# Moving eight bias-strip transfers to SyncE's queue and rolling the head iterations into loops, in a fused encoder layer

## The chip, the cores and the metric

The kernel runs on one core of a Trainium2 chip. Time is device microseconds of a whole execution. Three runs of the kernel before took 2651.68, 2651.73 and 2653.3 us, median 2651.73. The engines are TensorE (PE), VectorE (DVE), ScalarE (ACT), GpSimd (POOL, unused here) and SyncE (SP, which only issues transfers).

## The reference

One layer is applied to two sequences, 512 and 256 tokens of width 2048 (768 tokens in all), with shared weights:

```python
h = rmsnorm(x, pre_norm_g)
proj = h @ w_in                      # 2048 x 13376
q, k, v, z_attn, z_ssm, xbc, dt_raw = jnp.split(proj, cuts, axis=-1)
o = dilated_attention(q, k, v, rel_bias_table)          # 16 heads of 128
attn_out = rmsnorm(o, attn_norm_g) * silu(z_attn)
ssm_out = ssd_branch(z_ssm, xbc, dt_raw, ...)           # 32 heads of 64, both directions
mix = concat([attn_out, ssm_out]) @ w_out               # 4096 x 2048
return x + rmsnorm(mix, post_norm_g)
```

The attention adds a bias per head that depends only on the distance of query and key. The SSD branch convolves its input over five tokens, applies SiLU, and scans in chunks of 128 tokens with decays.

## The kernel before, in words

All products run in two parts: each float32 operand is split into a high part, rounded by ScalarE's copy (`w_hi`, `h_hi`), and the rest, which VectorE gets by a subtraction (`w_lo`, `h_lo`). TensorE adds three products, high by high, high by low and low by high. A weight chunk is four 128 x 128 blocks; it passes through `w_raw` (loaded by SyncE's queue), ScalarE (`split_hi`, line 933), VectorE (`split_lo`, line 1375) and TensorE, in four slots.

The stages, in order:

- The input is normalised and transposed, and a table of biases by distance is multiplied out and stored to `brow_scr` in DRAM (line 374).
- The B/C stage: one tile for `dt` and eight tiles of B and C, in a loop over groups.
- The gate stage: 48 column tiles of gates and x. Four go tile by tile; the other 44 form 22 pairs (`NP`), each computed by a Strassen-like scheme of seven block products. A product has two halves, so a pair has 14 halves (`HP`); one is 4 x 3 matmuls of 384 columns. Each pair needs four raw loads of 512 KB (`load_raw`, line 403: `raw_a` in `stage`, `raw_b` to `raw_d` in `raw_qk`). The third step of VectorE's pair work (line 1761) needs `raw_b` and `raw_d`. Results go out as two stores, `c1` (line 408, from `w_raw`) and `c2` (line 413, from `osq_sum`). ScalarE may overwrite `c2_buf` in the snapshot of its step n = 6 only after the `c2` store of the pair before has landed (line 1230).
- The head iterations: 16 rounds (`iteration`), each with 12 chunks of v, q and k columns of one head on TensorE, and between them, in `slot` and `step`, the attention and SSD work of the head before. TensorE runs these rounds from a loop of two, ScalarE and VectorE from unrolled code. The waits count up with the head number, so in a loop they compare with a value that is computed from a register.
- The tail: the last head's attention and SSD without a projection beside it (`step(s, HEADS - 1, None)`), with the first pieces of the output projection (`w2_split`, `m_split_first`) between its steps; then the output projection and the final norm.

Every engine works through its own list in order. Nothing reorders it: a wait holds all that is behind it on that engine. SyncE and ScalarE each issue transfers to a queue of their own.

Before head 0 starts, each head needs a strip: 128 rows of 896 biases, row r shifted by r. `make_strips(h)` (line 1239) makes two heads' strips by one DRAM to DRAM transfer from `brow_scr` to `strip_scr`. ScalarE issues eight of them, one behind each of the pairs 0 to 7, and these pairs are unrolled on ScalarE (lines 1244 to 1249).

In the last iteration (head 15), VectorE copies the columns of head 15's parameters (`columns_of_channels`, `columns_of_heads`) and convolves its x (`convolve_xs`) at the end of step 11 (line 1820), and ScalarE applies SiLU there (line 1271). In step 11 stand the splits of k (`k_hi`, line 946; `k_lo`, line 1583), in step 10 the gated output `y` of the head before (`y_gated`, line 1691) and the six transfers that follow it on ScalarE's queue.

Of the kernel before, what the change touches and what calls it, by code (L numbers as in the profile page):

```python
# [24 lines left out]
P = 128  # L25
# [44 lines left out]
STRIP = SEQ + 3 * P  # L70
# [26 lines left out]
W_TURNS = {24: (0,), 27: (1,), 31: (2, 3)}  # L97

# [23 lines left out]
def encoder(nc, x_prompt, x_sample, pre_g, w_in, rel_table, attn_g, conv_w, conv_b, dtb_f, dtb_b,  # L122
# [7 lines left out]
    with ctx:  # L130
# [137 lines left out]
        strip_out = sem("strip_out")  # L268
# [68 lines left out]
        def _(sp):  # L337
# [37 lines left out]

            sp.wait_ge(xt_done, 2 * KT)
# [6 lines left out]
            for c in range(2, NCH):  # L383
                load_w(2 * NCH + c, COL_C, c)
            with sp.Fori(1, SSM_GROUPS) as g:
                gcol = sp.snap(g * P)
                for j, base in enumerate((COL_B, COL_C)):
                    for c in range(NCH):
                        load_w(NCH + 2 * NCH * g + NCH * j + c, gcol + base, c)
# [42 lines left out]
            with sp.Fori(1, NP - 1) as p:  # L432
                pair_transfers(p)
# [481 lines left out]
        def _(act):  # L915
# [169 lines left out]
            def step(s, a, i, ip=0):  # L1085
                if a is None and s == 0:
                    act.wait_ge(pads, 3)
                    load_xs(0)
                    act.wait_ge(strip_out, 16 * (HEADS // 2))
                    load_strip(0)  # L1090
                    load_gate(za, ZX_ZA, 0, za_in)
                    load_gate(zs, ZX_ZS, 0, zs_in)
                    load_decays(0)
# [145 lines left out]
            def make_strips(h):  # L1239
                act.dma_start(strip_scr[h * P:(h + 2) * P, :],  # L1240
                              bass.AP(brow_scr.tensor, h * BROW + P - 1, [[BROW, 2], [-1, P], [1, STRIP]])
                              ).then_inc(strip_out, 16)

            for p in range(HEADS // 2):
                pair(p, p % 2)
                make_strips(2 * p)
            with act.Fori(HEADS // 4, NP // 2) as g:
                pair(2 * g, 0)
                pair(2 * g + 1, 1)
# [15 lines left out]
            def iteration(i, ip, a, final=False):  # L1265
                for s in range(IT_CHUNKS):
# [4 lines left out]
                    if final and s == 11:  # L1271
# [3 lines left out]
            for i in range(1, HEADS):  # L1275
                iteration(i, i % 2, i - 1, final=(i == HEADS - 1))
# [69 lines left out]
        def _(dve):  # L1346
# [467 lines left out]
            def iteration(i, ip, a, final=False):  # L1814
                for s in range(IT_CHUNKS):
# [4 lines left out]
                    if final and s == 11:  # L1820
# [7 lines left out]
            for i in range(1, HEADS):  # L1828
                iteration(i, i % 2, i - 1, final=(i == HEADS - 1))
# [21 lines left out]
            for s in range(IT_CHUNKS):  # L1851
                step(s, HEADS - 1, None)
                if s == 1:
                    w2_split(0)
# [125 lines left out]
```

## Time and profile before

| quantity | value |
|---|---|
| median of three runs | 2651.73 us |
| profiled execution | 2651.68 us |
| its span | 2649.9 us |
| TensorE busy | 2531.5 us (96%) |
| VectorE busy | 1541.0 us (58%) |
| ScalarE busy | 865.2 us (33%) |
| mean granted TensorE clock | 0.978 |
| chain that ended last | TensorE 89%, DMA 5%, VectorE 3% |

The span runs from the first to the last instruction. The busy shares are averages over stages with different limits, so they do not say what one stage waits for. The chain follows the end of the span back from wait to wait. In the rows below, L is the line of the kernel, the engine names are PE, DVE, ACT and SP, a q behind an engine name is its sequencer or transfer queue, and x is a count. A granted clock of 1.00 is 2.4 GHz and 0.50 is 1.2 GHz.

### The profile page before, as it was taken

Reading aid. Unit: us, or ns where it says so; the run is one execution under the profiler, and the core shown is the slowest. Engines: PE = TensorE matmul, PEld = TensorE weight load, DVE = VectorE, ACT = ScalarE, POOL = GpSimd, SP = SyncE. Lnnn points to the kernel's source line nnn. Section 1 sums busy time; section 2 is a strip of 40 time slices with the busy share of each in tenths; the row PEclk is TensorE's granted clock in tenths of the full one; section 3 lists DMA queues with packets and bytes.
Section 4 is the critical chain, followed back from the end, with each engine's and each line's share of the span. In section 5 each row is a group of like instructions: output and inputs, shape, how many; then the busy total and the mean of one; then the engine's idle time right before and its main releaser. Section 6 shows DMA issues by size and latency. Waiting matters only on the chain.

```text
span 2649.9 us, 36450 instructions
## 1 busy us (share of the span) xinstructions
PE 2531.5 (96%) x14004; PEld 2371.0 (89%) x14004; DVE 1541.0 (58%) x2389; ACT 865.2 (33%) x1410; POOL 0.2 (0%) x4
## 2 busy tenths in 40 slices
PE   6999877888999999999999999999999799999998
PEld 6999877888999999999999999999999688888887
DVE  5556644344555553566666666666666855544447
ACT  5232322223333332433333333333333422211112
POOL 0000000000000000000000000000000000000000
PEclk9999988989999999999999999999999899999999
DMA  5224222333333336244444444444444342222215
GB/s 178 79 99 136 71 92 95 104 94 99 101 93 96 102 103 209 73 147 145 146 146 146 146 146 146 146 146 146 146 146 134 134 149 88 87 85 101 85 61 200
DMA packets 287861, 320.94 MB, mean 121 GB/s; under 512 B 15031, under 2 KB 232311, under 8 KB 283304
## 3 DMA queue, kind: packets, MB, share of 16 engines
q1 hardware_dynamic: 252855, 196.87, 24.3%
q10 hardware_dynamic: 34928, 123.10, 13.2%
q8 instruction: 41, 0.67, 0.1%
q14 instruction: 37, 0.30, 0.0%
HBM read 271.76 MB, written 55.51 MB: 124 GB/s over the span
## 4 chain that ended last, share of the span: by engine, by line
PE 89%; DMA 5%; DVE 3%; ACT 1%; issue 1%; ACTq 0%; SPq 0%; DVEq 0%
PE ps L587 30%; PE ps L785 21%; PE ps L856 19%; PE ps L567 8%; DMA raw_qk<-in_w_in 5%; PE ps L713 2%; PE ps L741 2%; PE ps L680 2%; PE ps L696 1%; PE ps L751 1%; PE ps L600 1%; DVE w_lo L1742 1%; PE ps L718 0%; DVE w_raw L1746 0%; PE ps L687 0%
## 5 line engine op out<-in xcount | busy, mean ns | idle before, releaser
L587 PE MATMUL ps<-h_hi,w_hi 128*128 128x384 f32 x1536 | 401.5, 342 | 3.3 <-issue 3.3
L587 PE MATMUL ps<-h_hi,w_lo 128*128 128x384 f32 x1536 | 391.5, 335 | 0.0
L587 PE MATMUL ps<-h_lo,w_hi 128*128 128x384 f32 x1536 | 391.5, 335 | 0.0
L1375 DVE TENSOR_TENSOR w_lo<-w_raw,w_hi 128x512 fp32r<-128x512 f32 x244 | 167.2, 690 | 340.5 <-ACT w_hi L933 335.7
L933 ACT ACTIVATE w_hi<-w_raw 128x512 fp32r<-128x512 f32 x240 | 150.2, 627 | 608.3 <-PE ps L587 383.6
L856 PE MATMUL ps<-h_hi 128*128 128x512 f32 x768 | 299.8, 390 | 1.7 <-issue 1.7
L856 PE MATMUL ps<-h_lo,h_hi 128*128 128x512 f32 x768 | 298.8, 389 | 0.0
L856 PE MATMUL ps<-h_hi,h_lo 128*128 128x512 f32 x768 | 298.8, 389 | 0.0
L587 PEld LDWEIGHTS ps<-h_hi,w_hi 128*128 128x128 f32 x1536 | 272.5, 188 | 8.1 <-issue 6.1
L587 PEld LDWEIGHTS ps<-h_hi,w_lo 128*128 128x128 f32 x1536 | 278.5, 188 | 0.0
L587 PEld LDWEIGHTS ps<-h_lo,w_hi 128*128 128x128 f32 x1536 | 277.7, 188 | 0.0
L785 PE MATMUL ps<-t_hi,w_hi 128*128 128x384 f32 x528 | 187.5, 355 | 65.9 <-DVE w_lo L1742 65.9
L785 PE MATMUL ps<-h_hi,w_hi 128*128 128x384 f32 x704 | 236.6, 336 | 2.7 <-DVE w_lo L1742 2.7
L785 PE MATMUL ps<-h_hi,w_lo 128*128 128x384 f32 x704 | 236.3, 336 | 0.0
L785 PE MATMUL ps<-h_lo,w_hi 128*128 128x384 f32 x704 | 236.1, 335 | 0.0
L1921 DVE SCALAR_TENSOR_TENSOR stage<-ps,coef,stage 128x512 f32<-128x512 f32 x168 | 123.7, 748 | 178.6 <-PE ps L856 178.6
L1742 DVE TENSOR_TENSOR w_lo<-raw_qk,w_hi 128x512 fp32r<-128x512 f32 x176 | 121.7, 691 | 154.4 <-ACT w_hi L1207 152.8
L785 PE MATMUL ps<-t_lo,w_hi 128*128 128x384 f32 x528 | 185.4, 351 | 0.0
L785 PE MATMUL ps<-t_hi,w_lo 128*128 128x384 f32 x528 | 185.2, 351 | 0.0
L856 PEld LDWEIGHTS ps<-h_hi 128*128 128x128 f32 x768 | 144.2, 188 | 31.6 <-issue 2.1
L856 PEld LDWEIGHTS ps<-h_hi,h_lo 128*128 128x128 f32 x768 | 144.1, 188 | 30.1
L856 PEld LDWEIGHTS ps<-h_lo,h_hi 128*128 128x128 f32 x768 | 144.2, 188 | 29.6
(228 smaller groups left out, 3888.3 us busy)
## 6 DMA issues: line engine op xcount, KB each, us to landing
w_raw<-in_w_in SPq DMA_DIRECT2D x240, 256.0 KB, 2.9
raw_qk<-in_w_in SPq DMA_DIRECT2D x66, 512.0 KB, 3.9
stage<-in_w_out SPq DMA_DIRECT2D x30, 1024.0 KB, 5.0
stage<-cb_scr ACTq DMA_DIRECT2D x16, 1664.0 KB, 13.4
stage<-loc_scr ACTq DMA_DIRECT2D x16, 1536.0 KB, 7.1
stage<-zx_scr ACTq DMA_DIRECT2D x32, 384.0 KB, 3.6
stage<-er_scr ACTq DMA_DIRECT2D x32, 384.0 KB, 9.4
u_scr<-stage ACTq DMA_DIRECT2D x32, 384.0 KB, 2.7
```

What stands on the lines that cost most here:

```text
L567: last = nc.tensor.matmul(ps[:, 2 * parity + b, 0:HALF_T], w, h[:, k * T + b * HALF_T:k * T + (b + 1) * HALF_T], start=(k == 0 and p == 0) ...
L587: last = nc.tensor.matmul(ps[:, 2 * parity + b, 0:HALF_T], w, h[:, k * T + b * HALF_T:k * T + (b + 1) * HALF_T], start=(k == 0 and p == 0) ...
L600: nc.tensor.matmul(ps[:, 4 + sc, :], bcT[0][:, sc * P:(sc + 1) * P], bcT[1][:, 0:SEQ], start=True, stop=True).then_inc(pcb_ready, 1)
L680: last = nc.tensor.matmul(ps[:, 4 + t, :], q[:, t * P:(t + 1) * P], k[:, 0:SEQ], start=(n == 0), stop=(n == 2))
L713: last = nc.tensor.matmul(ps[:, 5, :], v_tok[:, b * P:(b + 1) * P], pT[:, b * SEQ:(b + 1) * SEQ], start=(b == 0), stop=(b == PCH - 1))
L741: last = nc.tensor.matmul(ps[:, b, o * P:(o + 1) * P], xsc[:, pr * P:(pr + 1) * P], cb[:, pr * P:(pr + 1) * P], start=(q == 0), stop=(q == ...
L785: ins = nc.tensor.matmul(ps[:, bank, 0:HALF_T], w, h(k), start=(start and kk == 0 and q == 0), stop=(last and kk == KC - 1 and q == 2), sk ...
L856: last = nc.tensor.matmul(ps[:, bank, :], m[par][:, k * T + t * P:k * T + (t + 1) * P], w[slot][:, k * NBW:(k + 1) * NBW], start=(k == 0 a ...
L933: nc.scalar.activation(w_hi[:, c, :], w_raw[:, c, :], ACT.Copy).then_inc(w_hi_done, 1)
L1375: nc.vector.tensor_tensor(w_lo[:, c, :], w_raw[:, c, :], w_hi[:, c, :].bitcast(f32), ALU.subtract).then_inc(w_lo_done, 1)
L1742: nc.vector.tensor_tensor(w_lo[:, n_slot(n, pp), :], src, w_hi[:, n_slot(n, pp), :].bitcast(f32), ALU.subtract).then_inc(w_lo_done, 1)
L1921: nc.vector.scalar_tensor_tensor(acc[:, o:o + NBW], ps[:, n % TT, :], r, acc[:, o:o + NBW], ALU.mult, ALU.add).then_inc(acc_added, 1)
```

## The change

Four things change.

1. `make_strips` becomes a function of SyncE. The first strip transfer is issued before the B/C loop, the other seven between the pair transfers of the gate stage, and for that the first eight pair transfers are unrolled on SyncE. The semaphore is split in two.
2. ScalarE's pair loop starts at pair 2 instead of pair 8.
3. The head iterations 1 to 14 become a loop of two on ScalarE and VectorE.
4. In the last iteration the column copies, the convolution and its SiLU move from step 11 to step 10; in the tail VectorE's `w2_split(0)` moves from step 1 to step 0.

```diff
+DVE_PER_PASS = 28
@@ semaphores
-        strip_out = sem("strip_out")
+        strip_out = [sem(f"strip_out{i}") for i in range(2)]
@@ SyncE
+            def make_strips(h, done):
+                sp.dma_start(strip_scr[h * P:(h + 2) * P, :],
+                             bass.AP(brow_scr.tensor, h * BROW + P - 1, [[BROW, 2], [-1, P], [1, STRIP]])
+                             ).then_inc(done, 16)
...
+            sp.wait_ge(brow_out, 16)
+            make_strips(0, strip_out[0])
             with sp.Fori(1, SSM_GROUPS) as g:
...
             pair_transfers(0)
-            with sp.Fori(1, NP - 1) as p:
+            for n in range(HEADS // 2 - 1):
+                make_strips(2 * n + 2, strip_out[1])
+                pair_transfers(n + 1)
+            with sp.Fori(HEADS // 2, NP - 1) as p:
                 pair_transfers(p)
@@ ScalarE, head 0
-                    act.wait_ge(strip_out, 16 * (HEADS // 2))
+                    act.wait_ge(strip_out[0], 16)
+                    act.wait_ge(strip_out[1], 16 * (HEADS // 2 - 1))
@@ ScalarE, pairs
-            for p in range(HEADS // 2):
-                pair(p, p % 2)
-                make_strips(2 * p)
-            with act.Fori(HEADS // 4, NP // 2) as g:
+            pair(0, 0)
+            pair(1, 1)
+            with act.Fori(1, NP // 2) as g:
@@ ScalarE and VectorE, last iteration
-                    if final and s == 11:
+                    if final and s == 10:
@@ ScalarE, iterations (VectorE's has in addition the counter of its own steps)
-            for i in range(1, HEADS):
-                iteration(i, i % 2, i - 1, final=(i == HEADS - 1))
+            with act.Fori(0, HEADS // 2 - 1) as g:
+                iteration(2 * g + 1, 1, 2 * g)
+                iteration(2 * g + 2, 0, 2 * g + 1)
+            iteration(HEADS - 1, 1, HEADS - 2, final=True)
@@ VectorE, tail
+                if s == 0:
+                    w2_split(0)
                 if s == 1:
-                    w2_split(0)
                     m_split_first(0)
```

On SyncE, from the raw loads of pair 0's transfers to the `c2` store of pair 0 (`zx_scr<-w_raw` is the `c1` store, `zx_scr<-osq_sum` the `c2` store), there stands before:

```order
L403 DMA stage<-in_w_in 128x8x128 [waits wsum_done]
L403 DMA raw_qk<-in_w_in 128x8x128 [waits w_lo_done] x3
L408 DMA zx_scr<-w_raw 128x768 [waits comb_done]
L432 UNCONDITIONAL_BRANCH
L413 ISA [waits c21_done]
L413 DMA zx_scr<-osq_sum 128x768
```

and now:

```order
L413 DMA stage<-in_w_in 128x8x128 [waits wsum_done]
L413 DMA raw_qk<-in_w_in 128x8x128 [waits w_lo_done] x3
L418 DMA zx_scr<-w_raw 128x768 [waits comb_done]
L380 DMA strip_scr<-brow_scr 256x1x896
L423 DMA zx_scr<-osq_sum 128x768 [waits c21_done]
```

The strip stands between the two stores, and the branch into the loop is gone from here.

On ScalarE, from the end of pair 0 to the snapshot of pair 1 that waits for `c2_out`, there stands before:

```order
L1207 ACTIVATE w_hi<-raw_qk 128x512 [waits half_done,raw_in_d] x2
L1240 DMA strip_scr<-brow_scr 256x1x896
L1207 ACTIVATE w_hi<-stage 128x512 [waits half_done,raw_in_a] x2
L1207 ACTIVATE w_hi<-w_raw 128x512 [waits half_done,wsum_done]
L1215 ACTIVATE osq_sum<-ps 128x384 [waits half_done]
L1207 ACTIVATE w_hi<-w_raw 128x512 [waits half_done,wsum_done]
L1207 ACTIVATE w_hi<-stage 128x512 [waits half_done,wsum_done]
L1211 ACTIVATE w_raw<-ps 128x384 [waits half_done,c1_out]
L1207 ACTIVATE w_hi<-stage 128x512 [waits half_done,wsum_done]
L1207 ACTIVATE w_hi<-raw_qk 128x512 [waits half_done,raw_in_c]
L1211 ACTIVATE osq_sum<-ps 128x384 [waits half_done,c2_out]
L1207 ACTIVATE w_hi<-raw_qk 128x512 [waits half_done,raw_in_c]
```

and now:

```order
L1221 ACTIVATE w_hi<-raw_qk 128x512 [waits half_done,raw_in_d] x2
L1221 ACTIVATE w_hi<-stage 128x512 [waits half_done,raw_in_a] x2
L1221 ACTIVATE w_hi<-w_raw 128x512 [waits half_done,wsum_done]
L1229 ACTIVATE osq_sum<-ps 128x384 [waits half_done]
L1221 ACTIVATE w_hi<-w_raw 128x512 [waits half_done,wsum_done]
L1221 ACTIVATE w_hi<-stage 128x512 [waits half_done,wsum_done]
L1225 ACTIVATE w_raw<-ps 128x384 [waits half_done,c1_out]
L1221 ACTIVATE w_hi<-stage 128x512 [waits half_done,wsum_done]
L1221 ACTIVATE w_hi<-raw_qk 128x512 [waits half_done,raw_in_c]
L1225 ACTIVATE osq_sum<-ps 128x384 [waits half_done,c2_out]
L1221 ACTIVATE w_hi<-raw_qk 128x512 [waits half_done,raw_in_c]
```

Only the strip transfer has left the list.

On VectorE, from the split of the last k tile into the tail (`h_lo<-w_raw` is `w2_split(0)`, 128x772 the convolution, the ISA rows the reduction of the scores with the bias), there stands before:

```order
L1583 SCALAR_TENSOR_TENSOR k_lo<-ps,k_hi 128x768 [waits qk_hi_done]
L1357 COPY cur<-conv_cols 128x5 [waits y_gated,ua_stored,ys_stored]
...
L1413 TENSOR_SCALAR stage<-stage,cur 128x772 [waits xs_in,dve_seq]
L1416 SCALAR_TENSOR_TENSOR stage<-stage,cur 128x772 [waits dve_seq] x4
L1607 ISA stage,cur<-ps,stage 128x512 [waits strip_in,scores_ready]
...
L1561 TENSOR_SCALAR stage<-stage 128x3072 [waits dve_seq]
L1618 RECIPROCAL cur<-cur 128x4 [waits probs_exp,sscores_ready]
...
L1630 TENSOR_SCALAR stage<-stage,cur 128x512 x3
L1833 TENSOR_TENSOR h_lo<-w_raw,h_hi 128x2048 [waits w2_hi_done]
```

and now:

```order
L1423 TENSOR_SCALAR stage<-stage,cur 128x772 [waits xs_in,dve_seq]
L1426 SCALAR_TENSOR_TENSOR stage<-stage,cur 128x772 [waits dve_seq] x4
L1593 SCALAR_TENSOR_TENSOR k_lo<-ps,k_hi 128x768 [waits qk_hi_done]
L1617 ISA stage,cur<-ps,stage 128x512 [waits scores_ready,strip_in,ua_stored,ys_stored]
...
L1571 TENSOR_SCALAR stage<-stage 128x3072 [waits dve_seq]
L1849 TENSOR_TENSOR h_lo<-w_raw,h_hi 128x2048 [waits w2_hi_done]
L1628 RECIPROCAL cur<-cur 128x4 [waits probs_exp,sscores_ready]
...
L1640 TENSOR_SCALAR stage<-stage,cur 128x512 x3
```

The convolution now precedes `k_lo`, and `w2_split(0)` precedes the sample's scores and the normalisation.

## Rows read from the trace of the kernel before

**Rows 1.** Busy time by stretch (column header in the first line), the gate stage's two parts.
```profile
core 0: us, PE busy (x) PEld busy (x) DVE busy (x) ACT busy (x) POOL busy (x), PEclk, DMA share, GB/s
302.00:612.00 310.00, 248.61 (x1320) 246.08 (x1320) 129.23 (x168) 81.14 (x145) 0.00 (x0) 0.89 0.31 97
612.00:1023.00 411.00, 408.67 (x2328) 408.35 (x2328) 221.53 (x293) 145.53 (x252) 0.00 (x0) 1.00 0.34 104
```

**Rows 2.** Chain of waits in time, gate stage: start us, length us, what.
```profile
320.64 15.08 DMA raw_qk<-in_w_in
...
612.64 408.67 PE ps L785 x2328
```

**Rows 3.** Waits, 300 to 620 us: total us, times, longest us.
```profile
PE ps L785 <- DVE w_lo L1742: 65.9, 9, 7.8
```

**Rows 4.** Timeline of ScalarE's queue, second strip: start us, length us, what.
```profile
357.94 0.61 ACTq L1240 DMA_DIRECT2D strip_scr<-brow_scr  x1
```

**Rows 5.** Busy time by stretch, while a strip moves: columns as in Rows 1.
```profile
336.00:338.00 2.00, 0.00 (x0) 0.00 (x0) 1.90 (x2) 0.94 (x3) 0.00 (x0) 0.54 0.13 53
...
341.00:342.00 1.00, 1.00 (x4) 1.00 (x4) 0.79 (x2) 0.66 (x2) 0.00 (x0) 0.50 0.12 51
```

**Rows 6.** Timeline of SyncE's queue, gate stage: start us, length us, what.
```profile
310.75 0.37 SPq L403 DMA_DIRECT2D stage<-in_w_in  x1
...
621.94 0.41 SPq L403 DMA_DIRECT2D stage<-in_w_in  x1
...
665.63 0.37 SPq L408 DMA_DIRECT2D zx_scr<-w_raw  x1
...
669.64 0.37 SPq L413 DMA_DIRECT2D zx_scr<-osq_sum  x1
...
680.59 0.41 SPq L403 DMA_DIRECT2D stage<-in_w_in  x1
```

**Rows 7.** Timeline of ScalarE, a pair without strip; in brackets the wait.
```profile
668.95 0.49 ACT L1215 ACTIVATE osq_sum<-ps 128x384 f32<-128x384 f32 x1 [0.84 <-PE ps L785]
...
677.32 0.49 ACT L1211 ACTIVATE osq_sum<-ps 128x384 f32<-128x384 f32 x1 [1.47 <-PE ps L785]
```

**Rows 8.** Timeline of VectorE, the same pair.
```profile
678.37 0.69 DVE L1742 TENSOR_TENSOR w_lo<-raw_qk,w_hi 128x512 fp32r<-128x512 f32 x1 [1.79 <-ACT w_hi L1207]
```

**Rows 9.** Timeline of SyncE's queue, first chunk load of the B/C loop.
```profile
62.98 0.39 SPq L359 DMA_DIRECT2D w_raw<-in_w_in  x1
```

**Rows 10.** Timeline of ScalarE, the same chunk's split.
```profile
78.79 0.63 ACT L933 ACTIVATE w_hi<-w_raw 128x512 fp32r<-128x512 f32 x1 [1.44 <-PE ps L567]
```

**Rows 11.** Chain of waits in time, B/C stage.
```profile
99.14 27.37 PE ps L567 x144
```

**Rows 12.** Timeline of ScalarE's queue, one head iteration.
```profile
1140.07 0.33 ACTq L1154 DMA_DIRECT2D u_scr<-stage  x1
```

**Rows 13.** Timeline of VectorE, the same iteration.
```profile
1144.88 0.96 DVE L1583 SCALAR_TENSOR_TENSOR k_lo<-ps,k_hi 128x768 fp32r<-128x768 f32 x1
```

**Rows 14.** Chain of waits in time, the same iteration.
```profile
1147.30 2.76 PE ps L680 x12
```

**Rows 15.** Timeline of VectorE, last iteration and tail.
```profile
2065.17 0.96 DVE L1691 TENSOR_TENSOR stage<-stage 128x768 f32<-128x768 f32 x1
...
2071.26 0.16 DVE L1357 COPY cur<-conv_cols 128x5 f32<-128x5 f32 x1
...
2076.80 0.68 DVE L1607 CUSTOM_DVE_ANT_0 stage<-ps,stage 128x512 f32<-128x512 f32 x1
...
2087.02 2.29 DVE L1833 TENSOR_TENSOR h_lo<-w_raw,h_hi 128x2048 fp32r<-128x2048 f32 x1
```

**Rows 16.** Timeline of ScalarE, the same stretch.
```profile
2069.55 0.81 ACT L946 ACTIVATE k_hi<-ps 128x768 fp32r<-128x768 f32 x1 [20.25 <-PE ps L587]
...
2076.92 0.63 ACT L958 ACTIVATE stage<-stage 128x512 f32<-128x512 f32 x1 [4.50 <-DVE stage L1416]
```

**Rows 17.** Timeline of TensorE, the same stretch.
```profile
2077.55 0.58 PE L687 MATMUL ps<-k_hi,q_hi 128*128 128x256 f32 x1 [3.11 <-DVE cur L1607]
```

More of the change, by code:

```diff
@@ L1237, in pair @@
                         t_hi_of(4, h_block(h_hi, 0, 1), h_block(h_lo_f, 0, 1))
[L1239 to L1242, printed above, removed]
-            for p in range(HEADS // 2):
-                pair(p, p % 2)
-                make_strips(2 * p)
-            with act.Fori(HEADS // 4, NP // 2) as g:
+            pair(0, 0)
+            pair(1, 1)
+            with act.Fori(1, NP // 2) as g:
                 pair(2 * g, 0)
@@ L1819, in iteration @@
                     step(s, a, i, ip)
-                    if final and s == 11:
+                    if final and s == 10:
                         dve.wait_ge(y_gated, i)
@@ L1827, in _ @@
             iteration(0, 0, None)
-            for i in range(1, HEADS):
-                iteration(i, i % 2, i - 1, final=(i == HEADS - 1))
+            start = seq[1]
+            with dve.Fori(0, HEADS // 2 - 1) as g:
+                seq[:] = [start + 2 * DVE_PER_PASS * g, 0]
+                iteration(2 * g + 1, 1, 2 * g)
+                iteration(2 * g + 2, 0, 2 * g + 1)
+                assert seq[1] == 2 * DVE_PER_PASS, seq[1]
+            seq[:] = [0, start + DVE_PER_PASS * (HEADS - 2)]
+            iteration(HEADS - 1, 1, HEADS - 2, final=True)
             def w2_split(u):
```

## The prediction, made before the changed kernel ran

> **What bounds the kernel now.** I read the chain of waits first: TensorE holds nearly all of it, so a gain must come from a place where TensorE waits. The busy time by stretch shows where that is. In the gate stage (lines 806 to 832, 22 column pairs) TensorE is busy 408.67 of 411 us in the later part but 248.61 of 310 us in the earlier part, at a mean granted clock of 0.89 instead of 1.00 [rows 1]. The chain of this stage has eight pieces like its first, about 15 us of waiting for a `raw_qk` load, and after 612.64 us one unbroken TensorE piece [rows 2]. The waits say the same: TensorE waited 65.9 us for `w_lo`, up to 7.8 us at a time [rows 3]. Eight is the number of strip transfers, and each is issued by ScalarE's queue behind a pair [rows 4]. A strip reads 256 rows of 3,584 bytes, 917,504 bytes. While one moves, the DMA engines are 12 to 13% busy at 51 to 53 GB/s: two of sixteen [rows 5]. At 51 GB/s it lasts 18.0 us. The weight load on SyncE's queue has a share on those two engines and creeps beside it.
>
> The Trainium skill (DMA: Bandwidth & Descriptors, Why a DMA increments its semaphore by 16) lets a DMA use at most the largest number up to 16 that divides the slowest dimension of both its patterns; here that is 2, and the share of the engines agrees.
>
> The price now: from the `raw_a` load at 310.75 to that of eight pairs later at 621.94 are 311.2 us, 38.9 a pair. Two pairs without strip take 680.59 - 621.94 = 58.65 us, 29.33 a pair [rows 6]. So a strip costs 9.57 us and eight cost 76.5. Some 7.8 us of each is standing still; the other 1.8 is work at half speed after the restart, where the granted clock is 0.50, the 1.2 GHz level [rows 5].
>
> **The change, part by part.** *Seven strips on SyncE's queue.* They are now issued behind the store of `c1`, and the store of `c2` stands behind them. `raw_d`, which each pair waited for, is issued and landed before: that stall goes. What is late next is the `c2` store. In a pair without strip the `c1` store is issued at 665.63, the `c2` store at 669.64 [rows 6]. The strip would be issued from 666.0 to 666.6 (0.61 us long [rows 4]). Its two engines have to move the share of `c1` first, so I let it begin at 668 (estimate; 666.6 is the earliest) and end at 686.0. If a queue is served in its order, the `c2` store's share on these two engines comes after: with 1.3 us for that (an estimate; the store of that size is issued and its buffer rewritten 677.32 - 669.64 = 7.7 us later without a wait, so it is below that) it lands at 687.3. ScalarE must have it before the snapshot that overwrites `c2_buf`, at 677.32 now [rows 7], and behind this snapshot on ScalarE's queue stand `w_hi` of half 7 and all later halves. `w_lo` of half 7 ends 678.37 + 0.69 - 677.32 = 1.74 us after the snapshot's start [rows 7, 8], so at 689.0. TensorE is due there at: the pair starts about 0.75 us before the 668.95 snapshot, 668.2, plus seven halves of 29.33 / 14 = 2.095 us, 682.9. It waits 6.1 us, then pays the 1.8 us of low clock: 7.9 us a pair, 55.3 for seven. Ends: a strip that begins at 666.6 with nothing behind it ends at 684.6 and gives 3.4 + 1.8, 36 in all; one that takes 21 us, as if loads ran beside it, gives 9.1 + 1.8, 76. I take 55.3, which has the strip alone on its engines as in the later of rows 5. Raw loads of the next pair are issued after the strip's end and keep their slack.
>
> *The first strip before the B/C loop.* It is issued ahead of the chunk load at 62.98 [rows 9], which then waits for two engines that may also carry the y12 stores of ScalarE's queue (lines 1044 to 1046). With 18 us of strip and, if the 3.1 MB of those stores interleave, their eighth part at the same 51 GB/s (7.7 us), it lands near 89. Its split is due at 78.79 [rows 10], so ScalarE stalls some 10 us, but TensorE takes up this chunk only at 99.14, after the cumulation [rows 11]. Nothing else of the dt chain stands behind. Cost 0, upper bound 3 us. This pair's 9.57 us vanish whole.
>
> Gate stage in sum: 76.5 - 55.3 = 21.2 us gained, between 0 and 40.
>
> *Loops instead of unrolled code.* ScalarE's pair loop now starts at pair 2; pairs 8 to 21 already ran rolled, at 29.33 us each, so 0. For the head iterations on ScalarE and VectorE the tightest place is the scores of the next slot: `y_gated`, six DMA issues on ScalarE from 1140.07 on [rows 12], `k_hi`, then `k_lo`, which ends at 1145.84 [rows 13]; TensorE comes at 1147.30 [rows 14]. Slack 1.46 us. A raw load costs 0.37 us to issue with a fixed address and 0.41 with one from a register [rows 6]; the register arithmetic ahead of it I bound by a whole issue more, 0.41. Six issues add 0.24 to 2.5 us. I take 0.9, near the lower end, and it stays covered: 0. If uncovered, each microsecond costs 14 us (14 rolled iterations).
>
> *The tail.* Before, `y_gated` of head 14 is done at 2066.13, VectorE idles until `k_lo`, then copies columns and convolves from 2071.26 to 2076.80, and only then takes the scores [rows 15]. Now the convolution (5.54 us) starts at 2066.2 and ends at 2071.8. But ScalarE's SiLU of it (0.63 us and a shorter piece, some 0.9 in all) now precedes `k_hi`, which starts at 2072.7 instead of 2069.55 [rows 16]; with 0.81 and 0.96 us for `k_hi` and `k_lo` TensorE gets its scores at 2074.5. They last 2.76 us at full clock [rows 14]. After 3.11 us of idle time TensorE restarted at the low clock (0.58 us for 256 columns [rows 17]), and now it idles five, so I count 2 us more: ready at 2079.3 instead of the 2076.80 at which VectorE used them, +2.5. Next, the first `w2_split` (2.29 us [rows 15]) moves ahead of the sample's scores and the normalisation, off a place where ScalarE's exponential covered it, onto the chain: +2.3. Behind it VectorE has no gap to give back. Sum +4.8, between +2.3 and +6.
>
> **Sum.** Against the profiled execution (2651.68 us, span 2649.9, 1.8 around it; the median of the runs is 2651.73): 2651.7 - 21.2 + 0 + 0 + 4.8 = 2635.3. I say 2635; its own range is 2614 to 2657 (both ends of the two terms).
>
> **Rivals.** *A, the store isn't held.* If the `c2` store passes the strip, all eight stalls go: 2651.7 - 76.5 + 4.8 = 2580. For it: fourteen of sixteen engines are free. Against: the store is complete only with all its shares. 12%.
>
> *B, the queue makes no difference.* The strip still holds two engines for 18 us and each of the seven pairs keeps its 9.57 us: 2651.7 - 9.6 + 4.8 = 2647. For it: the stall bound reaches there. Against: the load that was waited for has landed by then. 14%. The Trainium skill (DMA: Bandwidth & Descriptors, Issuing engines are not separate DMA queues) says that which engine issues only saves issue time, since all run on the same sixteen; that rule alone would give B. The same page (Queues, rings and completion order) has each DMA engine alternate between queues and take one queue's descriptors in order, which gives my forecast.
>
> *C, slower: the rolled head iteration.* Register arithmetic before the six issues and the waits of the `y_gated` to `k_lo` chain exceeds 1.46 us. At 2.5 us for the issues and one more issue's length (0.4) for the waits 1.44 stay exposed, times 14 is 20: 2655. It decides from 16.4 / 14 = 1.2 us exposed. Against: in the pair loop ScalarE and VectorE run rolled with TensorE unbroken [rows 2]. 12%. The Trainium skill (Runtime: NRT & Kernel Launch, Instruction fetch mechanics) warns that a taken branch out of the fetched window stalls the engine; no row here prices such a stall, and it would fall at the end of an iteration.
>
> **How the numbers follow.** My forecast 60%, A 12, B 14, C 12, and 2 for a stall in the B/C stage (2640). The range 2600 to 2657 leaves out A and a part of C. About 0.2%, 5.3 us, is what can be told from no change: faster (below 2646.4) is the forecast but for its upper edge (54), A, a part of B (5) and 2: 73%. Same: 18%, the rest of B, that edge and half of C. Slower: 9%.
>
> **What would show it.** Right: pairs 1 to 7 at about 37 us, TensorE waiting 6 us at half 7 (not at half 4) of each, ScalarE's `c2` snapshot waiting for `zx_scr<-osq_sum`, whose landing grows to about 17 us; no wait in the B/C stage; head iterations as far apart as before; the tail's scores reduced at about 2.5 us later and L696's transposes 4.8 later relative to `y_gated`. Wrong: pairs at 29.3 us (A) or at 38.9 (B), or TensorE idle before L680 in every iteration (C).

## The result, and the profile after

The changed kernel took 2687.37 us (median, 2686.34 to 2691.48) beside 2652.52 us for the kernel before: ratio 1.0132, 95% interval 1.0114 to 1.0149. It is slower by 1.3%; I had said 2635, 0.6% faster. Its profiled execution took 2686.07 us, with a span of 2684.3 us against 2649.9 and a mean granted clock of 0.973 against 0.978. Lines below are those of the changed kernel: L785 has become L798, L587 L600, L1211 L1225, L1375 L1385, L1583 L1593, L1691 L1701; line 1839 is VectorE's new loop.

Where the 34.4 us of span come from, by places that both traces have:

| stretch | before | after | difference |
|---|---|---|---|
| up to the gate stage's first product | 0 to 304.15 | 0 to 304.26 | +0.1 |
| from there to the start of the head iterations | 304.15 to 1024.59 | 304.26 to 1004.00 | -20.7 |
| start of head iterations to `y_gated` of head 14 | 1024.59 to 2065.17 | 1004.00 to 2093.90 | +49.3 |
| that `y_gated` to the end | 584.7 | 590.4 | +5.7 |

So the gate stage and the tail did what I had forecast (-21.2 and +4.8), and the head iterations, which I had put at nothing, cost 49 us.

The gate stage by stretch, answering [rows 1]:

```profile
302.00:572.00 270.00, 229.21 (x1212) 227.00 (x1212) 116.64 (x153) 75.41 (x135) 0.00 (x0) 0.92 0.31 99
572.00:1000.00 428.00, 427.73 (x2433) 427.73 (x2434) 230.63 (x307) 149.92 (x261) 0.00 (x0) 0.99 0.34 104
```

Its chain, answering [rows 2], and its waits, answering [rows 3]:

```profile
327.58 17.55 DMA zx_scr<-osq_sum
...
364.82 17.82 DMA zx_scr<-osq_sum
...
572.27 428.45 PE ps L798 x2436
1000.72 3.28 issue
```

```profile
ACT osq_sum L1225 <- DMA zx_scr<-osq_sum: 80.6, 7, 12.0
PE ps L798 <- DVE w_lo L1752: 43.5, 8, 6.0
```

There are seven such pieces now, one for each strip on SyncE's queue, and they are `c2` stores instead of `raw_qk` loads. ScalarE waits up to 12.0 us for them at its snapshot, and TensorE 6.0 us (I had said 6.1). SyncE's queue in one pair, answering [rows 6], and the landing of its transfers (KB each, median us from issue to landing):

```profile
360.83 0.36 SPq L418 DMA_DIRECT2D zx_scr<-w_raw  x1
361.23 0.64 SPq L380 DMA_DIRECT2D strip_scr<-brow_scr  x1
364.82 4.67 SPq L423 DMA_DIRECT2D zx_scr<-osq_sum  x1
385.86 0.39 SPq L413 DMA_DIRECT2D stage<-in_w_in  x1
```

```profile
zx_scr<-w_raw SPq DMA_DIRECT2D x1, 384.0 KB, 2.6
zx_scr<-osq_sum SPq DMA_DIRECT2D x1, 384.0 KB, 17.8
```

Two stores of one size on one queue: the one ahead of the strip lands after 2.6 us, the one behind it after 17.8.

The first strip, ahead of the B/C loop: ScalarE's split and TensorE's next chunk, answering [rows 10, 11]:

```profile
88.29 2.12 ACT L946 ACTIVATE w_hi<-w_raw 128x512 fp32r<-128x512 f32 x3 [10.89 <-DMA w_raw<-in_w_in]
```

```profile
100.10 26.52 PE ps L580 x144
```

ScalarE stands 10.9 us, and TensorE takes up the chunk at 100.10 with no idle time ahead of it.

Now the head iterations. First the chain of waits where one pass of VectorE's loop ends and the next begins:

```profile
1191.37 0.06 DVEq L1839
1191.43 7.55 issue
1198.98 0.09 DVEq L1839
...
1199.95 4.13 issue
1204.17 0.06 DVE cur L1367
```

L1839 is the loop's own line, so the first row is VectorE's branch, and "issue" is time in which the engine waits for nothing that the profile shows. The waits from 1090 to 2030 us count them:

```profile
DVE w_lo L1385 <- issue: 46.4, 6, 8.7
DVE cur L1367 <- issue: 25.7, 12, 4.4
```

Neither row exists before. Six is the number of times that a loop of seven passes branches back. TensorE meets it at the sample's scores (L700), which wait for VectorE's reduction of the first scores:

```profile
PE ps L700 <- DVE cur L1617: 38.0, 6, 6.9
```

This row does not exist before either. It is 6.3 us for each branch; behind it TensorE goes on at a granted clock of 0.71 from 1205 to 1212 us, which is where the rest of the 49.3 us can lie. VectorE's timeline at that seam, and then in the middle of the same pass, where the same instructions follow one another without a branch:

```profile
1190.86 0.96 DVE L1593 SCALAR_TENSOR_TENSOR k_lo<-ps,k_hi 128x768 fp32r<-128x768 f32 x1
1199.13 0.69 DVE L1385 TENSOR_TENSOR w_lo<-w_raw,w_hi 128x512 fp32r<-128x512 f32 x1 [7.31 <-issue]
...
1204.17 0.15 DVE L1367 COPY cur<-skip_cols 128x1 f32 x1 [4.22 <-issue]
...
1264.76 0.96 DVE L1593 SCALAR_TENSOR_TENSOR k_lo<-ps,k_hi 128x768 fp32r<-128x768 f32 x1
1267.44 0.69 DVE L1385 TENSOR_TENSOR w_lo<-w_raw,w_hi 128x512 fp32r<-128x512 f32 x1 [1.72 <-ACT w_hi L946]
```

The register arithmetic is there at both places; the 7.3 and 4.2 us only behind the branch. The DMA queues show what moves meanwhile (packets, MB, share of 16 engines; the windows are 1194 to 1197, 1201 to 1205 and 1215 to 1925 us):

```profile
q14 instruction: 2, 0.02, 2.2%
q14 instruction: 2, 0.02, 1.4%
q14 instruction: 25, 0.20, 0.1%
```

Last the tail, answering [rows 15 to 17]: VectorE, ScalarE, TensorE.

```profile
2093.90 0.96 DVE L1701 TENSOR_TENSOR stage<-stage 128x768 f32<-128x768 f32 x1
...
2102.22 0.96 DVE L1593 SCALAR_TENSOR_TENSOR k_lo<-ps,k_hi 128x768 fp32r<-128x768 f32 x1 [1.70 <-ACT k_hi L959]
2108.10 0.69 DVE L1617 CUSTOM_DVE_ANT_0 stage<-ps,stage 128x512 f32<-128x512 f32 x1 [4.92 <-PE ps L693]
```

```profile
2101.40 0.79 ACT L959 ACTIVATE k_hi<-ps 128x768 fp32r<-128x768 f32 x1
```

```profile
2103.23 0.75 PE L693 MATMUL ps<-k_hi,q_hi 128*128 128x512 f32 x1 [5.05 <-DVE k_lo L1593]
...
2120.68 3.47 PE L709 MATMUL ps<-sq_c,stage 128*128 128x128 f32 x16 [10.84 <-DVE stage L1640]
```

From `y_gated` to the reduction are 14.2 us (11.6 before), to the transposes of L709 26.8 us (22.0 before): +2.6 and +4.8, against +2.5 and +4.8 forecast. TensorE restarts on the scores after 5.05 us of idle time with a first product of 0.75 us (0.50 before), at the low clock (0.55 granted from 2103 to 2106 us).

### The profile page after: what moved, and what is told of

Its sections match the earlier page's. It is cut to its first block, busy times and chain, and to the rows that moved or that the text cites. A ratio compares the mean times of both kernels' runs of the same rounds, so it can differ in the third digit from the quotient of the medians.

```text
span 2684.3 us, 37398 instructions
## 1 busy us (share of the span) xinstructions
PE 2545.7 (95%) x14004; PEld 2385.2 (89%) x14004; DVE 1542.5 (57%) x2389; ACT 872.6 (33%) x1416; POOL 0.2 (0%) x4
## 4 chain that ended last, share of the span: by engine, by line
PE 85%; DMA 5%; issue 4%; DVE 3%; ACT 1%; ACTq 1%; SPq 0%; DVEq 0%
PE ps L600 27%; PE ps L798 21%; PE ps L869 19%; PE ps L580 8%; DMA zx_scr<-osq_sum 5%; PE ps L726 2%; PE ps L754 2%; PE ps L693 1%; PE ps L709 1%; PE ps L700 1%; PE ps L764 1%; PE ps L731 1%; PE ps L613 1%; PE ps L740 0%; PE ps L878 0%
## 5 line engine op out<-in xcount | busy, mean ns | idle before, releaser
L600 PE MATMUL ps<-h_hi,w_hi 128*128 128x384 f32 x1536 | 404.2, 344 | 3.3 <-issue 3.3
L600 PE MATMUL ps<-h_lo,w_hi 128*128 128x384 f32 x1536 | 394.1, 337 | 0.0
L600 PE MATMUL ps<-h_hi,w_lo 128*128 128x384 f32 x1536 | 393.2, 337 | 0.0
L1385 DVE TENSOR_TENSOR w_lo<-w_raw,w_hi 128x512 fp32r<-128x512 f32 x244 | 166.5, 690 | 366.5 <-ACT w_hi L946 313.8
L798 PE MATMUL ps<-h_hi,w_hi 128*128 128x384 f32 x704 | 243.7, 346 | 41.5 <-DVE w_lo L1752 41.5
L600 PEld LDWEIGHTS ps<-h_hi,w_hi 128*128 128x128 f32 x1536 | 274.9, 190 | 8.1 <-issue 6.1
L600 PEld LDWEIGHTS ps<-h_hi,w_lo 128*128 128x128 f32 x1536 | 280.5, 189 | 0.0
L600 PEld LDWEIGHTS ps<-h_lo,w_hi 128*128 128x128 f32 x1536 | 280.0, 190 | 0.0
L798 PE MATMUL ps<-h_hi,w_lo 128*128 128x384 f32 x704 | 242.0, 344 | 0.0
L798 PE MATMUL ps<-h_lo,w_hi 128*128 128x384 f32 x704 | 241.9, 344 | 0.0
L798 PE MATMUL ps<-t_hi,w_hi 128*128 128x384 f32 x528 | 181.1, 343 | 4.7 <-DVE w_lo L1752 4.7
L798 PE MATMUL ps<-t_lo,w_hi 128*128 128x384 f32 x528 | 180.5, 342 | 0.0
L798 PE MATMUL ps<-t_hi,w_lo 128*128 128x384 f32 x528 | 180.3, 342 | 0.0
L798 PEld LDWEIGHTS ps<-h_hi,w_hi 128*128 128x128 f32 x704 | 136.8, 194 | 44.1 <-DVE w_lo L1752 44.1
## 6 DMA issues: line engine op xcount, KB each, us to landing
stage<-cb_scr ACTq DMA_DIRECT2D x16, 1664.0 KB, 14.2
```

The lines of the kernel that those rows point to most:

```text
L600: last = nc.tensor.matmul(ps[:, 2 * parity + b, 0:HALF_T], w, h[:, k * T + b * HALF_T:k * T + (b + 1) * HALF_T], start=(k == 0 and p == 0) ...
L798: ins = nc.tensor.matmul(ps[:, bank, 0:HALF_T], w, h(k), start=(start and kk == 0 and q == 0), stop=(last and kk == KC - 1 and q == 2), sk ...
L1385: nc.vector.tensor_tensor(w_lo[:, c, :], w_raw[:, c, :], w_hi[:, c, :].bitcast(f32), ALU.subtract).then_inc(w_lo_done, 1)
```

## The experiments

All start from the changed kernel or the kernel before, as each says. "Rolled" means from a loop, "written out" unrolled. Single letters (F, S, R, and so on) are the theories that each expectation names. Rows of a loop are lines of the program's order, in which equal neighbours are put together and register arithmetic is left out, so they measure its length only roughly. The kernel before, measured beside them, had medians of 2652.8 to 2653.7 us.

### Which part costs what

**VectorE's iterations written out** in the changed kernel.

```diff
-            with dve.Fori(0, HEADS // 2 - 1) as g:
-                seq[:] = [start + 2 * DVE_PER_PASS * g, 0]
-                iteration(2 * g + 1, 1, 2 * g)
-                iteration(2 * g + 2, 0, 2 * g + 1)
+            for i in range(1, HEADS):
+                iteration(i, i % 2, i - 1, final=(i == HEADS - 1))
```

> The changed kernel with VectorE's head iterations 1 to 14 written out again; ScalarE's stay a loop. The trace of the changed kernel shows six stalls of VectorE at the start of a pass of its loop (7.3 to 8.7 us before the first w_lo, about 4 us more after the second column copy), and 16 KB more of instruction packets than usual in each. Theory F (the taken branch out of VectorE's loop must fetch code): all six stalls go, 49 us, so 2687.4 - 49 = 2638, and some 20 instruction packets fewer per... six passes. Rival R (register arithmetic inside the rolled VectorE code is what costs): 2638 as well; this run does not tell R from F, the next group does. Rival S (ScalarE's rolled loop holds VectorE up): 2687, the stalls stay.

Measured: 2636.81 us (ratio to before 0.9938, 0.9921 to 0.9954), and no wait of VectorE put down to "issue" in the iterations. That is within 2 us of the time that I had predicted for the whole change. Of the miss of 52 us, 50.6 lie in VectorE's loop.

**ScalarE's iterations written out**, VectorE's rolled (the same edit on the other engine).

> The changed kernel with ScalarE's head iterations written out again; VectorE's stay a loop. F: 2687, no change, because ScalarE's seam shows no gap in the trace (w_hi starts 0.02 us after the table load) and it waits 14 us for VectorE there. S: 2638.

Measured: 2682.52 us (1.0110, 1.0093 to 1.0127). The stalls are all there (this is VectorE's split, two lines further up in this kernel):

```profile
DVE w_lo L1383 <- issue: 44.6, 6, 7.7
```

S falls. The 4.9 us less than the changed kernel were not expected. Two of the changed kernel's six seams (the places where one pass ends and the next begins) have a first part of 8.90 and 8.70 us in the chain, where in this run all six lie between 7.28 and 7.92; that is some 2.5 us of it, and the rest stays open.

**Strips alone** (iterations and tail as before) and **tail alone** (on the kernel before).

> Only the strips on SyncE's queue and ScalarE's pair loop from pair 2; iterations and tail as before. By the two traces the gate stage is 20.6 us shorter and the B/C stage unchanged: 2652.5 - 20.6 = 2632. Rival: the loops on the other engines changed the time of the gate stage too, then it is off by more than 3 us.

> The kernel before with only the tail's edits (convolution, column copies and SiLU at step 10, w2_split(0) at step 0). By the two traces the last stretch is 5.7 us longer: 2652.5 + 5.7 = 2658. Rival: part of the 5.7 comes from code fetched late behind the loop's exit; then the edit alone costs my predicted 4.8 or less, 2656 to 2657.

Measured: 2632.78 us (0.9916, 0.9899 to 0.9932) and 2658.72 us (1.0024, 1.0014 to 1.0033). Against before these are -20.4 and +5.6; with the 50.6 that lie between the changed kernel and the one with VectorE written out the sum is +35.8, measured +34.9. The terms add up to within 1 us.

### What in VectorE's loop it is

**Four iterations in a pass**, so that twelve stay rolled but two branches are taken in place of six.

```diff
+            with dve.Fori(0, 3) as g:
+                seq[:] = [start + 4 * DVE_PER_PASS * g, 0]
+                for j in range(1, 5):
+                    iteration(4 * g + j, j % 2, 4 * g + j - 1)
```

> The changed kernel with four head iterations in a pass of VectorE's loop: three passes for iterations 1 to 12, and 13 to 15 written out. Twelve iterations stay rolled with the same register arithmetic, but only two branches are taken. F (each taken branch costs about 8.2 us): 2636.8 (iterations written out) + 2 x 8.2 = 2653. R (the rolled code is slower by itself, 49 us over 14 iterations): 2636.8 + 12 x 3.5 = 2679.

Measured: 2652.57 us (0.9999, 0.9990 to 1.0009). F said 2653, R 2679. The chain has two long pieces, one for each branch:

```profile
1324.73 7.31 issue
...
1597.09 6.39 issue
```

So here the price goes with the branches taken, 7.9 us each, and rolled code by itself has none that shows.

**The seam moved** from the end of step 11 to the end of step 4.

```diff
+            iteration(1, 1, 0, steps=range(5))
+            with dve.Fori(0, HEADS // 2 - 2) as g:
+                iteration(2 * g + 1, 1, 2 * g, steps=range(5, IT_CHUNKS))
+                iteration(2 * g + 2, 0, 2 * g + 1)
+                iteration(2 * g + 3, 1, 2 * g + 2, steps=range(5))
```

> The changed kernel with the seam of VectorE's loop moved from the end of step 11 to the end of step 4; a pass is again two iterations, now with five taken branches. F: the stall of about 7.5 us, and one of 4 us behind it, move to step 5, where VectorE in the trace waits 3.3 us and 1.6 us for other engines anyway, and where TensorE needs its result only some 5 us later. So TensorE loses 0 to 4 us in a pass in place of 8.2: 2637 to 2657. If the price of a branch does not depend on what stands behind it: 2637 + 5 x 8.2 = 2678.

Measured: 2636.17 us (0.9938, 0.9921 to 0.9955). The time fits F, but not for the reason that I gave: the stall did not move, it went. VectorE has no "issue" wait at any seam, and no packet of instructions comes on this queue from 1215 to 1925 us, where the changed kernel has 25. Five branches are taken without a fetch. So the branch alone is not the cause either, and my theory was incomplete.

**Longer loops in the gate stage** (VectorE's iterations written out): four pairs in a pass, 187 rows of the order, and ten pairs, 462 rows, where two pairs have 94.

```diff
-            with dve.Fori(1, NP // 2) as g:
-                pair(2 * g, 0)
-                pair(2 * g + 1, 1)
+            with dve.Fori(0, 20 // k) as g:
+                for j in range(k):
+                    pair(k * g + 2 + j, j % 2)
```

> Iterations of VectorE written out (2636.8 us), and VectorE's loop of the gate stage with four pairs in a pass (187 rows of the order) in place of two (94). A loop of 94 rows shows no stall and no instruction packets from pass to pass, one of 248 rows does. F asks for a limit of size between: either 187 rows still fit (no packet between the first pass and the stage's end, no idle VectorE at the seam, 2637) or they don't (four to five packets of 8 KB at each of four seams, and VectorE standing still for 5 to 8 us at each).

> The same with ten pairs in a pass (462 rows), one taken branch. F: packets and a stall of VectorE at this one seam, shorter than the 7.5 + 4 us of the head stage if the fetch queues behind data there (the DMA engines are 35% busy here, 90% there); TensorE loses 0 to 8 us once. If the stall belonged to something in the head iterations and not to the size of the loop: no stall at all, 2637.

Measured, one execution each: 2636.93 and 2637.25 us. With 187 rows there is no packet from 480 to 1000 us and no stall. With 462 rows there are eight packets and one stall of VectorE, at the seam:

```profile
706.36 0.69 DVE L1752 TENSOR_TENSOR w_lo<-stage,w_hi 128x512 fp32r<-128x512 f32 x1 [5.26 <-issue]
```

TensorE does not feel it: its chain runs on in one piece from 573.53 to 1001.72 us. So the effect is not tied to the head iterations, and a stall need not cost anything where it falls. Whether the 187 rows escaped by their length or by their place, this pair of runs does not say. The busy time by stretch, first during this stall and then during the first part of the changed kernel's at 1191 us:

```profile
700.00:706.30 6.30, 6.30 (x38) 6.30 (x37) 1.07 (x2) 1.63 (x3) 0.00 (x0) 1.00 0.33 93
```

```profile
1191.40:1199.00 7.60, 7.60 (x42) 7.09 (x41) 0.42 (x1) 2.11 (x3) 0.00 (x0) 1.00 0.98 327
```

The DMA share is 0.33 where the stall is 5.3 us, and 0.98 where it is 7.3. That fits a fetch that takes longer behind busy DMA engines, but two places don't show it.

**The same loop, elsewhere in the code.** The changed kernel's loop has 240 rows; the one with the moved seam had 236 and began 19 rows later, so either its length or its place could have freed it. To tell length from position the loop was left as it is, and small writes were put ahead of it, in VectorE's idle time of iteration 0, which comes before the loop.

```diff
                     step(s, a, i, ip)
+                    if a is None and s < 8:
+                        for _ in range(3):      # 3, 7, 11, 16: 24, 56, 88, 128 in all
+                            settle()
+                            did(nc.vector.memset(mx[:, 0:1], 0.0))
...
+            settle()
             start = seq[1]
```

> The changed kernel with 24 small writes of VectorE added to its head iteration 0 (in idle time), so that its loop stands 24 instructions later in the code; the loop itself is unchanged (240 rows). With the seam moved to step 4 the body had 236 rows and began 19 rows later, and it neither stalled nor fetched. Theory P (position: whether the loop's start is still held when the branch comes depends on where the loop lies against blocks of 128 instructions, the 8 KB packets): one of the three shifts 24, 56, 88 frees the loop, 2637 and no packets after the first pass; the others stay at 2687. Theory L (a limit of length between 236 and 240 rows, wherever the loop lies): all three stay at 2687 with four packets at each seam.

> As the one with 24, with 56 writes. P: either 2637 with no packets from pass to pass, or 2687; L: 2687.

> As the one with 24, with 88 writes. P: either 2637 with no packets from pass to pass, or 2687; L: 2687.

> The changed kernel with 128 writes in VectorE's iteration 0, and one wait ahead of its loop as in the kernels with 24, 56 and 88. Theory P with the period of a packet (8 KB, 128 instructions): the loop stands again as in the changed kernel, so six stalls and four packets at each seam, 2687. If the period is longer (two packets), or the wait ahead of the loop is what freed it: 2635, no packets from pass to pass.

> The changed kernel with only that wait ahead of VectorE's loop and no writes. P: the position is the same to within an instruction, so 2687 with six stalls (unless the edge lies just there). Rival W, the wait itself changes how the loop is entered: 2635.

Measured, one execution each:

| instructions ahead of the loop | time, us | packets, 1215 to 1925 us |
|---|---|---|
| 0, the changed kernel | 2687.37 | 25 |
| 0, with the last `settle` alone | 2684.30 | 25 |
| 24 | 2635.22 | 0 |
| 56 | 2637.29 | 0 |
| 88 | 2632.67 | 0 |
| 128 | 2688.02 | 25 |

With 24, VectorE at the first seam; with 128, the chain at the same place:

```profile
1189.73 0.96 DVE L1593 SCALAR_TENSOR_TENSOR k_lo<-ps,k_hi 128x768 fp32r<-128x768 f32 x1
1192.44 0.69 DVE L1385 TENSOR_TENSOR w_lo<-w_raw,w_hi 128x512 fp32r<-128x512 f32 x1 [1.75 <-ACT w_hi L946]
```

```profile
1190.23 7.61 issue
...
1198.82 4.39 issue
```

L falls: the same body stalls or not by where it lies. W falls: the wait alone frees nothing, and the stalled kernel with 128 writes has it too. P stands in its main point: the loop's place decides, and a shift by 128 instructions brings all six stalls back. These 128 are one packet: over the whole execution the queue carries 50 packets with the last `settle` alone and 51 with the 128 writes. That the pattern repeats every 128 instructions is not shown, though. 24, 56 and 88 lie 32 apart, so a period of 32 or 64 would give the same table, and no shift between was tried. P had said that one of the three shifts would free the loop; all three did. That the changed kernel lay at a bad place was chance.

### The gate stage

**All strips in one transfer**, behind pair 0 on ScalarE's queue and with the heads outermost (kernel before otherwise).

```diff
-                act.dma_start(strip_scr[h * P:(h + 2) * P, :],
-                              bass.AP(brow_scr.tensor, h * BROW + P - 1, [[BROW, 2], [-1, P], [1, STRIP]])
+                act.dma_start(strip_scr[:, :],
+                              bass.AP(brow_scr.tensor, P - 1, [[BROW, HEADS], [-1, P], [1, STRIP]])
```

> The kernel before, but all 16 heads' strips go in one transfer, issued by ScalarE behind pair 0, with the heads as the slowest dimension (16 in place of 2). Same bytes in all, 7.3 MB. If a transfer takes as many engines as its slowest dimension allows, this one takes all sixteen at about 8 x 51 = 408 GB/s, 18 us in all, once: seven of eight stalls of 9.57 us go and the one left is 0 to 20 us: 2652.5 - 76.5 + (0 to 20) = 2576 to 2596. If two engines still carried it, it would take 144 us and the pairs under it 38.9 us: 2640 or more.

Measured: 2589.16 us (0.9759, 0.9743 to 0.9775). One wait is left, and then one unbroken piece:

```profile
320.32 20.13 DMA raw_qk<-in_w_in
343.75 615.18 PE ps L785 x3504
```

Eight times the bytes of a strip pair moved in 29.0 us from issue to landing, beside loads and a store; two engines at 51 GB/s would have needed 144.

**The same transfer ahead of the B/C loop**, on SyncE's queue.

> The kernel before with all strips in one transfer of 16 heads, issued by SyncE ahead of the B/C loop, and none behind the pairs. The single transfer behind pair 0 left one wait of 20 us for the raw load (2589.2 in all). Here the chunk load behind it may wait 18 us, as it did behind the changed kernel's first strip without any cost. My theory: all eight stalls gone, 2652.5 - 76.5 = 2576. Rival: all sixteen engines are taken, where the first strip took two, and other loads of this stretch come late too: TensorE stands 5 to 15 us, 2581 to 2591.

Measured: 2575.37 us (0.9705, 0.9689 to 0.9722), the rival's price not paid. ScalarE waits 18.1 us for the chunk load, TensorE does not, and the gate stage has no stall at all:

```profile
95.64 2.82 ACT L937 ACTIVATE w_hi<-w_raw 128x512 fp32r<-128x512 f32 x4 [18.10 <-DMA w_raw<-in_w_in]
```

```profile
304.32 640.22 PE ps L789 x3648
944.54 3.28 issue
```

This gives the stage's length without strips, 304.32 to 947.82 = 643.5 us. Before it took 720.4, so eight strips cost 76.9 us (I had 76.5); after, 699.7, so seven cost 56.2 (I had 55.3).

**The strip behind the `c2` store** (only the strips changed, on SyncE's queue, in two-engine shape).

```diff
                 if not isinstance(p, int) or p > 0:
                     store_c2(p - 1)
+                if strips is not None:
+                    make_strips(strips, strip_out[1])
```

> As the kernel with only the strips on SyncE's queue (2632.8), but each strip is issued behind the c2 store in place of ahead of it. If the queue serves each engine in order, the snapshot no longer waits for c2, and the next pair's raw loads stand behind the strip on the two engines: the strip runs from about 670 to 688 in the pair's frame, where raw_a is issued at 680.6, so it lands near 690 and is needed only about 10 us later: the seven stalls of 7.9 us go, 2632.8 - 55 = 2578, up to 2595 if the last raw load is late. If order within the queue doesn't matter (the strip holds two engines for whoever comes): 2633.

Measured: 2575.51 us (0.9707, 0.9691 to 0.9723), 57 us less than with the strip ahead of the store. The same seven transfers, two engines each, cost almost nothing when they stand one place later: the gate stage lasts 644.1 us (304.43 to 948.57), 0.6 more than without strips. What now comes late are the raw loads behind the strip, `raw_a` 13.0 us after its issue where it took 4.1. ScalarE waits for them up to 4.1 us at a time and VectorE up to 2.5, but TensorE has work enough ahead. SyncE's queue:

```profile
357.96 0.36 SPq L423 DMA_DIRECT2D zx_scr<-osq_sum  x1
358.36 0.61 SPq L380 DMA_DIRECT2D strip_scr<-brow_scr  x1
368.39 0.39 SPq L413 DMA_DIRECT2D stage<-in_w_in  x1
```

### The last two

**The changed kernel repaired**: 24 instructions ahead of the loop, strips behind `c2`, the tail's edits undone.

> The changed kernel with its three costs taken away, each in the way that an earlier run pointed to: the strips stand behind the c2 store (the 55 us), VectorE's loop stands 24 instructions later (the 50 us), and the tail's edits are undone (about 5 us). ScalarE's and VectorE's iterations stay rolled. If the terms are independent it equals the written-out kernel with the strips behind c2, 2575.5; if rolled code has a price of its own beside the branch, it is more than 2580.

**The convolution early, its SiLU late**, on the kernel with one strip transfer ahead of the B/C loop.

```diff
@@ VectorE only
-                    if final and s == 11:
+                    if final and s == 10:
```

> The fastest version so far (one strip transfer ahead of the B/C loop, 2575.4) with VectorE's column copies and convolution of the last iteration at step 10, while ScalarE's SiLU stays at step 11 behind k_hi. In the trace with both early, k_hi waited for the SiLU and TensorE's scores then ran at half clock, 2.3 us late. Theory: with the SiLU behind k_hi the scores start 1 to 1.4 us later than before (k_lo behind the convolution), but VectorE is free when they end, so the reduction moves by -1 to +1: 2574 to 2577. Rival: the gap of TensorE passes into the half clock anyway, +2: 2577.5.

Measured: 2574.18 us (0.9704, 0.9688 to 0.9720) and 2574.91 us (0.9705, 0.9689 to 0.9721). The first shows rolled iterations on both engines at the time of the written-out ones (2575.51). The second can't be told from its base (2575.37). In its trace the reduction comes 12.3 us after `y_gated`, against 11.7 in its base and 14.2 in the changed kernel: most of the changed kernel's 2.6 us (by which its reduction came later than before) come from the SiLU ahead of `k_hi`.

## Why the prediction was wrong

**The step that failed** is "Loops instead of unrolled code": "Six issues add 0.24 to 2.5 us. I take 0.9 ... and it stays covered: 0." The register arithmetic was as small as said: from the first of ScalarE's six issues to the split behind them it is 3.73 us, where before it was 3.44 (1140.07 to 1143.51), and `y_gated` to `k_lo` grew from 5.80 to 6.24 us, within the slack of 1.46.

```profile
1259.67 0.36 ACTq L1168 DMA_DIRECT2D u_scr<-stage  x1
...
1263.40 0.63 ACT L946 ACTIVATE w_hi<-w_raw 128x512 fp32r<-128x512 f32 x1 [6.57 <-issue]
```

But it was the only cost that I priced. The term was 0 and measured 49.3 us in the traces, 50.6 by the run with VectorE written out.

**Rival C** had the right sign but the wrong mechanism, place and size: it put the price on the chain from `y_gated` to `k_lo`, 14 times. It falls six times, on VectorE, behind the branch. Beside it stood the sentence of the Trainium skill that gives the real one (Runtime: NRT & Kernel Launch, Instruction fetch mechanics): a taken branch whose target is outside the fetched window stalls the engine. I set it aside because no row priced it and "it would fall at the end of an iteration". That was the error in reasoning: the end of an iteration is where `k_lo`, the scores' reduction and the sample's scores follow one another, and I had myself called the scores of the next slot the tightest place. My sign for C, TensorE idle before the scores (L680) in every iteration, did not come either: it idles before the sample's scores, six times. And the evidence that I used against C, loops of the pair stage that run without a stall, came from bodies of 94 and 76 rows, not 240.

The same section of the Trainium skill says that the small instruction memory of most engines is 32 KiB, 512 instructions, filled in blocks of 256. If it kept the last 512, a body of 240 rows would stay inside at any place and cost nothing. The measurements decide otherwise: 8 KB packets, a refetch in every pass at one place and again 128 instructions later, none at three places between. The 64 bytes for an instruction that follow from its figures agree with the one packet more for 128 writes. Five packets in a pass are then 640 instructions, far more than the body; why so many are fetched, no run shows.

**Gate stage**: right, in its mechanism and its size. Strips: 76.5 forecast for before, 76.9 measured; 7.9 forecast for each of seven after, 8.0 measured; the `c2` store was to land 687.3 - 669.64 = 17.7 us after its issue and took 17.8; TensorE's wait 6.1, measured 6.0. The pair shown takes 37.7 us (348.17 to 385.86 between `raw_a` loads), forecast 37. Rival B's rule, that the queue makes no difference, falls with the strip behind `c2`. What the Trainium skill says of queues (DMA: Bandwidth & Descriptors, Queues, rings and completion order), that each DMA engine takes one queue's descriptors in order, agrees with both places of the strip. Ahead of `c2`, the two stores take 2.6 and 17.8 us; behind it, `c2` takes 2.6 and the raw load that follows the strip 13.0. Rival A (no store held) is what happens there, though by order and not because a store passes. That begin (668) and share (1.3 us) of the forecast came out to 0.1 us is partly luck: both were estimates. **First strip**: right, 0 us, with ScalarE standing 10.9 us. **Tail**: right, +4.8 us to the transposes. The whole stretch gives +5.7; the other 0.9 were not followed up. **The chances** were added up wrongly: by their own parts (9 + 6 + 6) "same" is 21%, not 18, and "slower" 6%, not 9.

The sum from the table, against the profiled execution: 2651.7 + 0.1 - 20.7 + 49.3 + 5.7 = 2686.1, measured 2686.07.

## What to carry to other kernels

Before a long body is rolled into a loop, count its instructions and ask what stands right behind the branch: a refetch cost 7.3 + 4.2 us of VectorE here, about 8.2 of the total time for each branch taken, and a neutral shift of the code by a few dozen instructions removed it. A wait of the looped engine put down to "issue" once in each pass, with instruction packets that go on throughout the loop, gives it away. Measure such a loop at two positions in the code before it is judged.

A transfer whose outermost dimension is two occupies two DMA engines, and what stands behind it in its queue lands late (17.8 us for a store that takes 2.6): put it behind the store that someone waits for, or give it an outermost dimension of sixteen. Either was worth 77 us here, 2.9%.

## What the runs showed of the hardware that was not expected

- A loop of VectorE of 240 rows fetched its code again in each pass, five packets of 8 KB, or never, depending on its place: as it lay and 128 instructions later it did, 24, 56 and 88 later it did not. A body of 187 rows at the one place tried did not; one of 462 did.
- ScalarE's and TensorE's loops of the head iterations showed no such stall at the places where they lay. Whether a shift would give them one was not tried.
- In the changed kernel the stall comes in two parts, 7.3 to 8.7 and about 4 us, each with two packets before its end.
- A transfer of 7.3 MB with 16 as its outermost dimension landed in 29.0 us in the gate stage and 35.5 us ahead of the B/C loop. There the DMA engines moved 356 GB/s from 64 to 84 us, ScalarE waited 18.1 us, and TensorE lost nothing.
